# ScalarE's order before the attention items, and another placement of the side work beside them

## The reference

```
def retention(q, k, v, g):                      # 4 chunks of 128 tokens
    scores = einsum('bhncd,bhnsd->bhncs', q, k) * dmask
    o_inner = einsum('bhncs,bhnse->bhnce', scores, v)
    ...                                         # state carried from chunk to chunk
    o = o * rsqrt(mean(o * o) + eps)
    return silu(g) * o

def nsa(...):                                   # per block of 128 queries
    pc = masked_softmax(q @ kc, mc)             # compressed keys: gelu(z @ w1 + b1) @ w2 + b2
    ps = masked_softmax(q @ k_selected)         # all 8 blocks of 64 keys are selected here
    pwin = masked_softmax(q @ k_window)
    return g0 * (pc @ vc) + g1 * (ps @ v_selected) + g2 * (pwin @ v_window)

mix = concatenate([y_ret, y_nsa]) @ w_out[l]
```

## Time and profile before

| | |
|---|---|
| median of 3 runs | 1375.25 us |
| the profiled execution | 1376.43 us, of which the span from first to last instruction is 1374.6 us |
| granted TensorE clock over the span | 0.998 |
| TensorE busy | 1349.0 us (98%) |
| VectorE, ScalarE, GpSimd busy | 728.0, 604.4, 699.3 us |
| the items of layer 0 | 200.69 us to about 297 us |
| the same items in layer 1 | 678.85 us later (item 0 starts at 879.54 us) |

### The profile page before, as it was taken

How to read it: one execution, slowest core, us unless ns; L and a number is a source line. 1 busy time by engine, 2 the same in 40 slices (tenths; PEclk the granted TensorE clock), 3 DMA queues, 4 the chain that set the end, 5 groups by cost and what they waited for, 6 DMA issues and landing times.

```text
span 1374.6 us, 17665 instructions
## 1 busy us (share of the span) xinstructions
PE 1349.0 (98%) x6888; PEld 1114.2 (81%) x6888; DVE 728.0 (53%) x910; ACT 604.4 (44%) x1041; POOL 699.3 (51%) x544
## 2 busy tenths in 40 slices
PE   9999999999999999999999999999999999999998
PEld 6889877778888888888888888777798888888886
DVE  5506659745554444644462075686455554556443
ACT  5233568645433333423442335676463333334221
POOL 2644678644544444544465446786544444445441
PEclk9999999999999999999999999999999999999999
DMA  5433320031323323322133334100333323323331
GB/s 206 138 100 108 116 84 16 1 123 62 123 92 97 102 93 95 101 95 92 62 123 107 114 93 138 37 11 1 123 102 100 105 93 92 105 95 93 98 101 61
DMA packets 34882, 127.18 MB, mean 93 GB/s; under 512 B 3952, under 2 KB 4464, under 8 KB 34416
## 3 DMA queue, kind: packets, MB, share of 16 engines
q1 hardware_dynamic: 34656, 125.53, 28.5%
q10 hardware_dynamic: 144, 0.52, 0.2%
HBM read 123.94 MB, written 2.10 MB: 92 GB/s over the span
## 4 chain that ended last, share of the span: by engine, by line
PE 86%; DVE 6%; ACT 4%; issue 2%; POOL 1%; DMA 1%; DVEq 0%; POOLq 0%; ACTq 0%; SPq 0%
PE bank L1769 33%; PE bank L1801 17%; PE bank L1419 17%; PE bank L1435 4%; PE bank L1663 3%; PE bank L1701 2%; ACT E L831 1%; DVE s_bias L1217 1%; PE bank L1630 1%; DVE pt_l L952 1%; PE bank L1523 1%; PE bank L1387 1%; PE bank L1728 1%; PE bank L1727 1%; POOL w_lo L554 1%
## 5 line engine op out<-in xcount | busy, mean ns | idle before, releaser
L554 POOL TENSOR_TENSOR w_lo<-raw,w_hi 128x1024 fp32r<-128x1024 f32 x216 | 521.3, 2419 | 472.9 <-ACT w_hi L655 472.5
L655 ACT ACTIVATE w_hi<-raw 128x1024 fp32r<-128x1024 f32 x220 | 230.9, 1054 | 242.5 <-DMA raw<-wstream 242.4
L1769 PE MATMUL bank<-act_hi,w_hi 128*128 128x512 f32 (+1 forms) x768 | 286.0, 372 | 0.6 <-DVE act_lo L952 0.6
L1769 PE MATMUL bank<-act_lo,w_hi 128*128 128x512 f32 (+1 forms) x768 | 285.2, 371 | 0.0
L1769 PE MATMUL bank<-act_hi,w_lo 128*128 128x512 f32 (+1 forms) x768 | 285.2, 371 | 0.0
L911 ACT ACTIVATE cv<-bank,par 128x512 f32<-128x512 f32 x88 | 68.6, 779 | 286.0 <-PE bank L1769 286.0
L1348 DVE SCALAR_TENSOR_TENSOR cv<-bank,par,cv 128x511 f32<-128x511 f32 x88 | 66.0, 750 | 225.3 <-ACT cv L911 225.3
L1769 PEld LDWEIGHTS bank<-act_hi,w_hi 128*128 128x128 f32 x768 | 144.7, 188 | 26.7 <-DVE act_lo L952 1.6
L1769 PEld LDWEIGHTS bank<-act_hi,w_lo 128*128 128x128 f32 x768 | 144.7, 188 | 25.1
L1769 PEld LDWEIGHTS bank<-act_lo,w_hi 128*128 128x128 f32 x768 | 144.7, 188 | 24.9
L1419 PE MATMUL bank<-w_hi,act_hi 128*128 128x512 f32 (+1 forms) x384 | 145.0, 377 | 0.0
(11 more groups left out here) (177 smaller groups left out, 2179.1 us busy)
## 6 DMA issues: line engine op xcount, KB each, us to landing
raw<-wstream SPq DMA_DIRECT2D x220, 512.0 KB, 3.6
g_all<-gains SPq DMA_DIRECT2D x2, 2048.0 KB, 6.9
x_out<-x SPq DMA_DIRECT2D x8, 256.0 KB, 2.0
x<-x_in SPq DMA_DIRECT2D x3, 512.0 KB, 9.0
const<-consts SPq DMA_DIRECT2D x1, 1030.0 KB, 13.7
g_all<-gains ACTq DMA_DIRECT2D x1, 512.0 KB, 5.4
x<-x_in SPq DMA_DIRECT2D x2, 256.0 KB, 5.4
par<-pars SPq DMA_DIRECT2D x2, 235.0 KB, 3.8
```

What stands on the lines that cost most here:

```text
L554: nc.gpsimd.tensor_tensor(w_lo[:, s, :], raw_slot(s), r32(w_hi[:, s, :]), ALU.subtract)\
L655: nc.scalar.activation(w_hi[:, s, :], raw_slot(s), ACT.Copy).then_inc(hi_ready, 1)
L1769: last = mm(bank[:, b, first:end], a, v, start=(k == 0 and n == 0), stop=(k == KD - 1 and n == 2), skip_group_check=True)
```

## The change

Only the order of work is changed; no operation is added or taken out of the computation. In `MIDDLE` the entry `("keep", 2)` goes behind `("turn", 3)`. `hidden(1)` goes ahead of the first exponentials on ScalarE and `turn_hidden(1)` ahead of the first job on TensorE; `queries_first(5)` goes one exponential earlier. The tables of the items get other numbers: among them `Q6_END`, `Q6_REST` from 3 to 1, one k-step of projection 7 from item 2 to item 1, job 18 from item 7 to 6, job 25 from 15 to 16, job 30 from 21 to 20, job 32 from item 25 to 24 (jobs 33 and 34 stay at 25), job 35 stays at 26, job 38 from 32 to 31, job 39 from 33 to 32, job 40 from 34 to 33, job 41 from 36 to 34, job 42 from 37 to 38, job 43 from 42 to 41, and the output projection's piece (1, 0) from 43 to 44. The weight chunks C_WO+1 and C_WO+2 are split at items 3 and 4 in place of 1 and 5.

```
-          ("k", 3), ("keep", 2), ("turn", 3), ("first", 3), ("hidden", 0), ("score", 3), ("norm", 2), ("second", 3),
+          ("k", 3), ("turn", 3), ("keep", 2), ("first", 3), ("hidden", 0), ("score", 3), ("norm", 2), ("second", 3),
...
-        Q7_AT = {0: (0, 1), 1: (1, 2), 2: (2, 3), 3: (3, 6), 5: (6, 8)}
-        Q6_END, Q7_END = 3, 6
-        Q6_REST, Q7_REST = 3, 6
-        OUT_COPY = (4, 3, 2, 5, 2, 3, 5, 4)
-        OUT_SUM = (5, 4, 3, 5, 5, 4, 5, 4)
+        Q7_AT = {0: (0, 1), 1: (1, 3), 3: (3, 6), 5: (6, 8)}
+        Q6_END, Q7_END = 1, 6
+        Q6_REST, Q7_REST = 1, 6
+        OUT_COPY = (2, 5, 2, 3, 3, 3, 2, 3)
+        OUT_SUM = (5, 5, 2, 5, 5, 5, 2, 4)
...
-        WO_CHUNK_AT = {1: C_WO + 1, 5: C_WO + 2, 11: C_WO + 3, 21: C_WO + 4, 26: C_WO + 5}
+        WO_CHUNK_AT = {3: C_WO + 1, 4: C_WO + 2, 17: C_WO + 3, 21: C_WO + 4, 25: C_WO + 5}
...
-                       10: (21, 23, 25, 25), 11: (25, 26, 27, 31), 12: (32, 33), 13: (34, 36), 14: (37,),
+                       10: (20, 23, 24, 25), 11: (25, 26, 27, 31), 12: (31, 32), 13: (33, 34), 14: (38,),
...
-                    if z == 1:
+                    if z == 0:
                         hidden(1)
-                    if z == 6:
+                    if z == 5:
                         queries_first(5)
...
+                    if n == 1:
+                        turn_hidden(1)
                     for z in EARLY_AFTER.get(n, ()):
                         job_scores(z)
-                    if n == 2:
-                        turn_hidden(1)
```

More of the change, by code:

```diff
@@ L340, in build @@
         CMP_BANK, CMP_AT = (7, 0), (0, 24)
-        Q7_AT = {0: (0, 1), 1: (1, 2), 2: (2, 3), 3: (3, 6), 5: (6, 8)}
-        Q6_END, Q7_END = 3, 6
-        Q6_REST, Q7_REST = 3, 6
-        OUT_COPY = (4, 3, 2, 5, 2, 3, 5, 4)
-        OUT_SUM = (5, 4, 3, 5, 5, 4, 5, 4)
+        Q7_AT = {0: (0, 1), 1: (1, 3), 3: (3, 6), 5: (6, 8)}
[3 more added lines that the diff above has]
+        OUT_SUM = (5, 5, 2, 5, 5, 5, 2, 4)
         Y_AT = (7, 10, 14, 17)
-        WO_AT = {26: [(0, 0)], 28: [(0, 1)], 30: [(3, 0)], 35: [(3, 1)], 37: [(2, 0)], 38: [(2, 1)],
-                 40: [(3, 2)], 43: [(3, 3), (1, 0)], 45: [(1, 1)], 47: [(2, 2), (2, 3)]}
+        WO_AT = {26: [(0, 0)], 28: [(0, 1)], 29: [(3, 0)], 34: [(3, 1)], 36: [(2, 0)], 37: [(2, 1)],
+                 40: [(3, 2)], 42: [(3, 3)], 44: [(1, 0)], 45: [(1, 1)], 46: [(2, 2)], 47: [(2, 3)]}
         ff_hi = lambda k: g_hi[:, k, :] if k < 2 else act_hi[:, (k - 2) % KD, :]
         ff_lo = lambda k: g_lo[:, k, :] if k < 2 else act_lo[:, (k - 2) % KD, :]
-        WO_CHUNK_AT = {1: C_WO + 1, 5: C_WO + 2, 11: C_WO + 3, 21: C_WO + 4, 26: C_WO + 5}
+        WO_CHUNK_AT = {3: C_WO + 1, 4: C_WO + 2, 17: C_WO + 3, 21: C_WO + 4, 25: C_WO + 5}
         query_tile = lambda v: (T - 1 - v % T, v // T)
@@ L380, in build @@
             last_user[slot] = n
-        UNIT_SCORES = {4: (4, 4), 5: (7, 7), 6: (8,), 7: (10,), 8: (12, 13, 14, 15), 9: (17, 18, 19, 20),
-                       10: (21, 23, 25, 25), 11: (25, 26, 27, 31), 12: (32, 33), 13: (34, 36), 14: (37,),
-                       15: (42,)}
+        UNIT_SCORES = {4: (4, 4), 5: (6, 7), 6: (8,), 7: (10,), 8: (12, 13, 14, 16), 9: (17, 18, 19, 20),
+                       10: (20, 23, 24, 25), 11: (25, 26, 27, 31), 12: (31, 32), 13: (33, 34), 14: (38,),
+                       15: (41,)}
         SCORES_AT = {}
```

## The result

The changed kernel takes 1379.96 us (median of 10 executions, 1376.97 to 1385.14) against 1375.08 us (10 executions, 1374.62 to 1376.47): ratio 1.0037 [1.0027, 1.0046]. It is slower by 4.9 us, where 4.4 us faster were forecast. The profiled execution took 1380.15 us, 3.72 us more than the profiled one of before.

The account below looks back on a forecast made before the run. TensorE, busy 98% of the span, was taken as the bound, so only its stops could change. Terms summed to -2.20 us per layer, -4.4 for two; 1376.43 - 4.4 - 1.18 = 1370.85 us, range 1367.8 to 1375.8.

Parts of the forecast that it names:

- Retention: Retention's last chunk: the stop for `kT` goes, a longer one for `qr` comes; +0.40 us per layer.
- the third rival: Retention's masked scores are not late: -1.0 for +0.40 us per layer, 1368.05 us; chance 0.08.
- Times are in before's clock: Whole count: all times and durations were taken at the clock of the kernel before; no size given.
- Early jobs and items 0 to 23: Per layer: early score jobs -1.30, items 0 to 2 -0.70, 3 to 10 -0.98, 11 to 23 +0.18 us.
- The first rival: Item 3 on: `c_rec` waits for both GpSimd splits, until 210.6; -1.1 us per layer, 1373.05 us; chance 0.09.
- the second: Items 0 to 18: VectorE keeps its own pace, early gains are waited out; +0.78 us per layer, 1376.8 us; chance 0.13.
- Items 24 to 27: Job 32 one item earlier shortens job 35's wait, job 34 waits 0.4 us; -0.55 us per layer, bounds 0 and -1.83.
- the lock: At `c_rec`: VectorE operations with two SBUF inputs and GpSimd operations block each other for a whole instruction; `c_rec` took 1.63 us.
- Items 31 to 35: Job 39 waits for its bank in item 32, a new stop of 1.4 us; +1.24 us per layer.
- The fourth rival: From item 32 ScalarE falls one item behind; jobs 40, 41 and piece (2, 0) wait too; 1379.25 us; chance 0.10.
- items 42 to 46: Piece (1, 0) no longer waits for job 43's exponentials; -0.49 us per layer.
- the walk: One layer counted engine by engine with before's durations and the new order, giving TensorE's start times; -2.20 us per layer.

Follow-up runs that it names:

- experiment 6: The kernel before with only the entries keep 2 and turn 3 swapped in `MIDDLE`: 1377.94 us, ratio 1.0016.
- experiment 7: The changed kernel with GpSimd's fifth weight chunk back at item 26 and VectorE's rest of projection 2 put behind `norm` 2: 1367.95 us, ratio 0.995.
- experiment 5: The kernel before with only the fifth weight chunk moved from item 26 to item 25: 1375.14 us, ratio 0.9999.
- the fourth experiment: The changed kernel with `MIDDLE` as before and the fifth weight chunk back at item 26: 1371.12 us, ratio 0.9974.
- 8: experiment 7 with jobs 39, 40, 41 an item later and pieces (2, 0), (2, 1) at items 37 and 38: 1366.08 us, ratio 0.9931.
- the third: The changed kernel with only `MIDDLE` as before: 1377.58 us, ratio 1.002.
- experiments 2: The changed kernel with only GpSimd's split of the fifth chunk back at item 26, ScalarE's copy left at 25: 1372.66 us, ratio 0.9991.
- experiment 1: The changed kernel with only the fifth weight chunk back at item 26 instead of 25: 1372.79 us, ratio 0.9989.

## Why the prediction was wrong, point by point

**Retention, right in size, wrong in what it leaves out.** The stop for `kT` went and one for `qr` came, as written, so the third rival is out. The changed kernel's rows:

```profile
154.07 0.59 ACT L745 ACTIVATE qT<-bank 128x512 f32<-128x512 f32 x1
154.55 0.60 ACT L745 ACTIVATE kT<-bank 128x512 f32<-128x512 f32 x1
155.03 2.44 ACT L773 ACTIVATE KH<-bank 64x512 fp32r<-64x512 f32 x4
...
156.61 1.16 PE L1498 MATMUL bank<-qT,kT 64*128 64x128 f32 x16
157.50 2.85 DVE L952 TENSOR_TENSOR KL<-bank,KH 64x512 fp32r<-64x512 f32 x4 [1.14 <-ACT KH L773]
161.58 0.68 DVE L1122 TENSOR_TENSOR qr<-bank,head_rstd 128x512 f32<-128x512 f32 x1
162.41 0.46 PE L1519 MATMUL bank<-state,qxT 128*128 128x128 f32 x2 [1.72 <-DVE qr L1122]
```

`KL` was put at 157.7 and came at 157.50; L1519 at 162.58, came at 162.41. What failed is the sentence "Times are in before's clock": one stop of 1.72 us had taken the place of two of 0.99 and 0.26, and the sum gave no price to a clock that falls behind it. By the mean clocks of experiment 6 that is about 1.8 us of the median (an estimate); experiment 7 takes the stop away and has 0.998.

**Early jobs and items 0 to 23, right.** One table load where three were (at 177.18), no stop at jobs 4 and 8 (181.58 and 188.04, forecast 181.2 and 187.8), item 2's turn at 202.68 and item 10's at 217.60 without a bracket. `c_rec`:

```profile
203.57 7.13 POOL L554 TENSOR_TENSOR w_lo<-raw,w_hi 128x1024 fp32r<-128x1024 f32 x3
...
207.26 1.13 DVE L1297 SCALAR_TENSOR_TENSOR c_rec<-c_rec,gate_inv 128x16 f32<-128x16 f32 x1
```

It was expected at about 0.7 us. It waited for one split of three and got in before the next. The first rival (it waits for all) is out, and so is the second: VectorE did not keep its own pace. Most of the 0.38 us missing is item 9, 1.22 us long, where before's 1.77 less the 0.85 forecast make 0.92.

**Items 24 to 27, the step that failed.** The bounds were 0 and -1.83; it came to +1.18 in layer 0. Without the collision it is 7.20 - 7.93 = -0.73 us, beside the -0.55 forecast, so the work on jobs 32 to 35 was right. What the step did not do is to set each small VectorE operation beside GpSimd's list, though the lock had been found, priced and watched at `c_rec` two parts above, and though the moved chunk brought a split of 2.4 us into item 25. L1252 had been 0.37 us long at most and was carried over as such. Yet before's own rows at item 25 have the sign in them:

```profile
249.23 0.74 POOL L627 TENSOR_TENSOR act_lo<-o_f,act_hi 128x256 fp32r<-128x256 f32 x1 [2.57 <-ACT act_hi L872]
...
249.63 0.37 DVE L1252 TENSOR_SCALAR c_stat<-c_stat 128x16 f32<-128x16 f32 x1
```

The same operation takes 0.17 us in experiment 5, where no GpSimd operation runs beside it. Here it takes 0.37 and ends at 250.00, 0.03 us after GpSimd's L627 (249.97). It was already colliding, with an operation of 0.74 us; the moved chunk put one of 2.37 us in that place.

**Items 31 to 35, right** (1.29 us by the bracket for job 39, item 32 at 2.96 for 1.51). The fourth rival, ScalarE an item behind, gives nearly the measured time (1379.25 us) for a wrong reason, and that is luck: job 40 waits not at all, job 41 0.20 us, piece (2, 0) 0.86 us. Items 31 to 35 take 10.56 us for 8.56, with one more job of 0.60 in them, so +1.40 for the +1.24 forecast. The -0.49 of items 42 to 46 came nearly: items 41 to 46, which hold job 43 in both kernels, take 12.24 us for 11.28 with one more piece of 1.38, so -0.42. Items 36 to 40, to which the walk gave nothing, have +0.25 (10.87 us for 11.22, with one job of 0.60 less); what makes it up was not traced.

**The sum.** From the fourth experiment to the changed kernel there are 1379.96 - 1371.12 = 8.84 us: twice 1.9 for the collision, 0.8 for the swap's order, and by the mean clocks (0.9946 over ten executions against 0.998 over eight) about 4.7 for the clock, 9.3 together. The last is an estimate. The forecast of 1370.85 us had neither the first nor the last. The changed kernel's ten times broadly follow their clocks, from 1376.97 us at 0.998 to 1385.14 at 0.991.

Open: why the clock falls behind a stop in some executions and not in others. That it is these stops is shown in so far as the stretches begin behind them, and are absent in the profiles of experiments 4, 7 and 8, which lack the stop ahead of `out` and the longer one at job 35. Against a plain rule stand two profiles: the first has the stop ahead of `out`, the third the one of 2.33 us at job 35, and neither has a stretch. The mean clock of an execution also holds what happens at its start: before's profile has a stretch at 1.2 GHz from 10.6 to 14.0 us and experiment 7's one of 6.8 us from 8.3, the changed kernel's has none there. So a difference of means says how much clock was lost, and not at which stop. Nor was a kernel tried that keeps the stop and fills it with matmuls.

## What to carry to other kernels

Where the order of work moves, lay VectorE's small operations from SBUF to SBUF beside GpSimd's long ones, at each place and not only where the profile of before shows the collision, and ask of each tenth of a microsecond which comes first. Count stops by their length, not by their sum: two short ones merged into one of 1.7 us cost 0.4 us a layer more by the walk, and by the clocks of experiment 6 about twice that on top. When a copy moves on one engine, move what hangs on it on the next engine too (experiment 7), or the wait comes back one step on.

## What was not expected of the hardware

- A `tensor_scalar` over 128x16 elements took 2.07 us beside a GpSimd split and 0.17 without; over 128x24 elements 2.25 and 0.16 us. Who starts first decides: the collision came with a start 0.15 us behind the split's, and not with one 0.11 us ahead. Over the ten profiles each L1252 and L1056 that started while a split or an L627 ran, 31 in all, ended 0.03 to 0.04 us after that operation. Beside L614 alone on GpSimd (128x2 elements, shown 0.70 us long) L1252 took its 0.17 us every time.
- Stretches of 3.4 and 6.8 us at 1.2 GHz in the middle of a TensorE that is busy 98% of the time, behind stops of 1.7 and 2.3 us. They came in the profiles of three kernels of the ten (the changed one, experiments 2 and 6) and cost about half their length.
- An edit with no effect of its own (experiment 5) and one that costs 7.2 us in company (experiment 1) are the same number in a table.
